# Output strips cut in half and moved in a two-block transformer kernel: half strips ahead of the last head's later sums, the third pair's transposes ahead of the last values

## The chip, the cores and the metric

The kernel runs on one core of a Trainium2 chip. The metric is the device time of one execution in microseconds. The compute engines run their own instruction streams in program order and meet at semaphores: PE (TensorE, matmuls and transposes), DVE (VectorE), ACT (ScalarE) and POOL (GpSimd). SyncE starts the transfers.

## The reference

The reference is a stack of blocks on `x` of 512 rows by 1024 columns. The first block has a convolution layer and a differential attention layer, each with a memory attention and a squared-relu MLP. Its result goes into a second block, where the change is made:

```python
def second_block(x, ...):
    a = _rmsnorm(h, g_pre_mix[l])
    u = jnp.einsum("bsd,dc->bsc", a, w_in[l])
    ...
    conv_out = _conformer_conv(c_val, c_gate, ...)      # GLU, 31 taps, layernorm, silu
    attn_out = _stick_breaking(q, k, v)                 # 8 heads of 64
    attn_out = _rmsnorm(attn_out, attn_norm_g[l]).reshape(B, S, SB_WIDTH)
    mixed = jnp.concatenate([conv_out, attn_out], axis=-1)
    y = jnp.einsum("bsc,cd->bsd", mixed, w_out[l])
    h = h + _rmsnorm(y, g_post_mix[l])
    ...                                                 # gated MLP, second residual

def _stick_breaking(q, k, v):
    # A[t,s] = sigmoid(z_ts) * prod_{s<j<t} (1 - sigmoid(z_tj)), s < t
    ...
    between = lax.cumsum(log_1m_beta, axis=3, reverse=True) - log_1m_beta
    attn = jnp.where(mask, jnp.exp(log_beta + between), 0.0)
    return jnp.einsum("bhqk,bhkd->bhqd", attn, vh)
```

## The kernel before

Every float32 product is made of three matmuls: each operand is split into a rounded high part and a rest, and `mm3` (lines 1060, 1061 and 1062) multiplies high by high, rest by high and high by rest. Matmul sums stand in eight PSUM banks of 128x512 float32.

In the second block the order of work is one list of steps, `PLAN_C`. PE, ACT and DVE each walk the same list, and each does its own share of a step. A step is a name and a number; the order on an engine is that of the list, and semaphores hold an engine where its step needs another's result. The eight heads are units 0 to 7, two heads make a pair. For unit u the steps are:

- `lg` logits on PE; ACT and DVE make the logarithms from them (ACT lines 2099 to 2103, DVE line 2801 in `sp`);
- `sl` ACT rounds the logarithms (line 2108), DVE takes the rest (line 2805);
- `bt` the later sums, `between`, on PE: 20 matmuls (line 1564), the first ten with the rounded part, the others with the rest, added onto the logits in their banks. Even units use banks 0 to 2, odd ones 3 to 5;
- `ex` ACT: exponentials of the three banks (line 2114), counted by semaphore `sb_exp`, three a unit;
- `ah`, `at` ACT rounds the weights (line 2120), DVE takes the rest (line 2809), counted by `at_lo`;
- `va` PE: 12 matmuls of `mm3` into bank 6 (the values); `kp` ACT keeps that head (line 2126) and, after a pair's second head, squares both (line 2130).

For pair p, `ps` sums the squares on PE (line 1617, two columns wide), `pr` and `px` make and spread the norm's factor, `pt` transposes it into bank 7 on PE (line 1622), DVE multiplies it in (line 2824), and `pl` splits the result (ACT line 2145, DVE line 2828, semaphore `pair_lo`).

The convolution's layernorm is woven in: `ln_qa` adds squares on DVE (line 2848), `ln_var` sums them over channels on PE (line 1632, semaphore `ln_q` ahead of it), `ln_mul 0` transposes the factor into bank 7 on PE (line 1637), `ln_mul 1` multiplies it into the four channel groups on DVE (line 2857, four instructions, each read of bank 7 counted by `ln_dve`, from 5 to 8), `silu` and `ll` finish a group.

The output product `w_out_2` is made of strips: a strip is one PSUM bank t (rows 128t to 128t+127), one slab of weights, and two of the eight groups of 128 channels. The first slab holds channel groups 4 and 5, which are pair 0 and pair 1. `o` does strips of that slab, six matmuls each, in banks 0 to 3; `os` those of the next slabs.

Bank 7 is used by several steps in turn. Each of them first waits until the one before has been read, in the order of the list:

```python
        def out_of_7(step):
            ...
            if kind == "pt":
                return S("pair_n"), step[1] + 1
            if kind == "ln_var":
                return S("rs_v"), USE["ln",] + 1
            return S("ln_dve"), 4 if kind == "ln_sub" else 8
```

Of the kernel before, what the change touches and what calls it, by code (L numbers as in the profile page):

```python
# [97 lines left out]
def build(nc, cols, ins, out):  # L98
    sems = {}

    def S(name):
        if name not in sems:
            sems[name] = nc.alloc_semaphore(f"s_{name}")
        return sems[name]
# [18 lines left out]
    banks = [nc.alloc_psum_tensor(f"ps{b}", [128, 512], F32) for b in range(8)]  # L123
# [169 lines left out]
    OUT_KS = [[4, 5], [0, 1], [2, 3], [6, 7]]  # L293
# [326 lines left out]
    PLAN_C = []  # L620
# [12 lines left out]
    for u in range(8):  # L633
# [39 lines left out]
        if u >= 4 and u % 2:  # L673
            PLAN_C += [("pl", u // 2 - 2)]
        PLAN_C += [("taps", 1 if u < 3 else 3)]
    PLAN_C += [("bt", 7), ("ln_qa", 3), ("ps", 2), ("ln_var",), ("va", 6), ("ex", 7), ("pr", 2), ("ln_rs",), ("px", 2),
               ("ah", 7), ("ln_mul", 0), ("at", 7), ("kp", 6), ("ln_mul", 1), ("o", (0, 1)), ("va", 7), ("silu", 0), ("ll", 0),
               ("o", (2,)), ("pt", 2), ("kp", 7), ("ps", 3), ("silu", 1), ("ll", 1), ("o", (3,)), ("silu", 2), ("pl", 2),
               ("ll", 2), ("silu", 3), ("ll", 3), ("w", SL["out", 0, 0] + 4), ("os", 0, 1, (0, 1, 2, 3)), ("pr", 3), ("px", 3),
               ("os", 0, 2, (0, 1)), ("pt", 3), ("pl", 3), ("os", 0, 2, (2, 3))]  # L680

# [201 lines left out]
    M2h, M2l = Ah, Al  # L883
# [163 lines left out]
    def tensor_program(e):  # L1047
        q = Lane(e)
        mm = e.matmul
        at = {"slab": 0}  # L1050

        def next_slab():
            i = at["slab"]
            at["slab"] += 1
            q.wait_ge(S("w_lo"), 2 * i + 2)
            return i, WH[i % N_SPLIT], WL[i % N_SPLIT]

        def mm3(ps, lh, ll, rh, rl, start, stop, skip=False):
            k = dict(skip_group_check=True) if skip else {}
            mm(ps, lh, rh, start=start, stop=False, **k)  # L1060
            mm(ps, lh, rl, start=False, stop=False, **k)  # L1061
            return mm(ps, ll, rh, start=False, stop=stop, **k)  # L1062
# [4 lines left out]
        def tile_t(xh, xl, job, bank, free, turn=no_step, step=no_step):  # L1067

            i, wh, wl = next_slab()
            for k in range(8):  # L1070
                if turn is not no_step:

                    a, k_ = slice(k * 128, k * 128 + 128), dict(skip_group_check=True)
                    q.wait_ge(S("turn_hi"), 8 * JOB[job] + k + 1)
                    if k == 0:
                        free()
                    mm(banks[bank][:, :], wh[:, a], xh[:, k, :], start=k == 0, stop=False, **k_)
                    mm(banks[bank][:, :], wl[:, a], xh[:, k, :], start=False, stop=False, **k_)
                    turn(k)
                    q.wait_ge(S("turn_lo"), 8 * JOB[job] + k + 1)  # L1080
                    m = mm(banks[bank][:, :], wh[:, a], xl[:, k, :], start=False, stop=k == 7, **k_)
                    continue
                q.wait_ge(S("turn_lo"), 8 * JOB[job] + k + 1)
                if k == 0:
                    free()
                m = mm3(banks[bank][:, :], wh[:, k * 128:k * 128 + 128], wl[:, k * 128:k * 128 + 128],
                        xh[:, k, :], xl[:, k, :], k == 0, k == 7)
                if k == 3:
                    step(0)
            m.then_inc(S("w_used"), 1)  # L1090
            step(1)
# [51 lines left out]
        def turn_in_tile(src, job):  # L1143
            return lambda k: turn_next(src, job, 4 + k) if k < 4 else None

        def spread(x, job):
            for t in range(4):
                q.wait_ge(S("rs_n"), 3 * USE[job] + 3)
                i = e.transpose(banks[7][:, 128 * t:128 * t + 128], rms(job, t, 1).broadcast_to([128, 128]), IDENT)
            i.then_inc(S("spread_ps"), 1)  # L1150
# [199 lines left out]
        held, in_use = [], {}  # L1350
# [127 lines left out]
        for p, slot in enumerate(B.plan):  # L1478
            if p == 1:
                row_turn(3, 0)  # L1480
            if p < len(PIECES):
                c, j, t = PIECES[p]
# [22 lines left out]
        def in_free(n):  # L1505
            if n < 4:
                q.wait_ge(*x_final(1, n))
            else:
                q.wait_ge(*in_done(IN_FIRST[n - 4]))

        def v2_slab(j):

            c = CH["v2"]
            _, wh, wl = next_slab()
            for t in range(4):
                if j == 0:
                    q.wait_ge(S("spread"), 4)
                a = slice(128 * t, 128 * t + 128)
                for r, k in enumerate(c.ks[j]):
                    w = slice(512 * r, 512 * r + 512)  # L1520
                    m = mm3(banks[4 + t][:, :], Ah[:, k, a], Al[:, k, a], wh[:, w], wl[:, w], k == 0, k == 7)
                if t == 3:
                    m.then_inc(S("w_used"), 1)
                elif j == 3:
                    m.then_inc(S("n_tile"), 1)

        def free_7(step):

            i = IN_7.index(step)
            if i:  # L1530
                q.wait_ge(*out_of_7(IN_7[i - 1]))
            else:
                q.wait_ge(S("vz_lo"), 4)
# [56 lines left out]
        def block_step(kind, *a):  # L1590
            step = (kind,) + a
            if step in IN_7:
                free_7(step)
            if kind == "tile":
                n = IN_FIRST.index(a[0]) if a[0] in IN_FIRST else -1
                tile_t(Ah, Al, "pre_mix", n % 4 if n >= 0 else 7, lambda: in_free(n) if n >= 0 else None,
                       turn_in_tile(X, "pre_mix") if n == 0 else no_step)
                if n == 0:
                    q.wait_ge(S("turn_lo"), 8 * JOB["pre_mix"] + 8)
                    spread(X, "pre_mix")  # L1600
            elif kind == "v2":
                v2_slab(a[0])
            elif kind == "lg":
                logits(a[0])
            elif kind == "bt":
                between(a[0])
            elif kind == "va":
                values(a[0])
            elif kind == "cv":
                conv_group(a[0])  # L1610
            elif kind == "o":
                out_first(a[0])
            elif kind == "ps":
                q.wait_ge(S("pair_sq"), a[0] + 1)
                q.wait_ge(S("keep"), 2 * a[0] + 2)
                for t in range(4):
                    m = mm(banks[6][:, 2 * t:2 * t + 2], OQ[:, 128 * t:128 * t + 128], HALF[:, :], start=True, stop=True)
                m.then_inc(S("pair_ps"), 1)
            elif kind == "pt":
                q.wait_ge(S("pair_b"), a[0] + 1)  # L1620
                for t in range(4):
                    m = e.transpose(banks[7][:, 128 * t:128 * t + 128], TN[:, 128 * t:128 * t + 128], IDENT)
                m.then_inc(S("pair_t"), 1)
            elif kind == "os":
                out_slab(*a)
            elif kind == "ln_sub":
                q.wait_ge(S("ln_s"), 3)
                mm(banks[7][:, :], ONES, T4[:, 0, :], start=True, stop=True).then_inc(S("ln_ps"), 1)
            elif kind == "ln_var":
                q.wait_ge(S("ln_q"), 7)  # L1630
                for t in range(4):
                    m = mm(banks[7][:, 2 * t:2 * t + 2], GL[:, 0, 128 * t:128 * t + 128], ONES[:, 0:2], start=True, stop=True)
                m.then_inc(S("ln_ps"), 1)
            elif step == ("ln_mul", 0):
                q.wait_ge(S("rs_n"), 3 * USE["ln",] + 3)
                for t in range(4):
                    m = e.transpose(banks[7][:, 128 * t:128 * t + 128], LNR[:, t:t + 1].broadcast_to([128, 128]), IDENT)
                m.then_inc(S("ln_ps"), 1)

        def mixed_ready(k):  # L1640
            if k < 4:
                q.wait_ge(S("mix_lo"), k + 1)
            else:
                q.wait_ge(S("pair_lo"), k - 3)
# [12 lines left out]
        def out_strip(w, j, n, t):  # L1657
            return strip(w, OUT_KS[j], t, 4 * n + t, M2h, M2l, mixed_ready, j == 0, j == 3)

        def out_first(tiles):  # L1660


            if not held:
                held[:] = next_slab()
            for t in tiles:
                q.wait_ge(S("sb_exp"), 21 if t < 3 else 24)
                m = out_strip(held, 0, 0, t)
                if t == 3:
                    m.then_inc(S("w_used"), 1)

        def out_slab(n, j, tiles):

# [25 lines left out]
        for step in PLAN_C:  # L1698
            block_step(*step)
# [37 lines left out]
        for n, j in DN[:3]:  # L1737
            w = next_slab()
            for t in range(4):
                m = down_strip(w, j, n, t)  # L1740
# [1274 lines left out]
```

## Time and profile before

| | |
|---|---|
| median of 3 runs | 1763.02 us (1762.97 to 1763.67) |
| the profiled execution | 1763.04 us |
| its span (first to last instruction) | 1761.2 us |
| PE busy | 1719.3 us, 98% of the span |
| DVE busy, ACT busy | 1256.6 us (71%), 818.4 us (46%) |
| chain that ended last | PE 89%, DVE 6%, ACT 3% |
| mean granted clock of PE | 0.993 |

Times in the rows are microseconds from the start of the span. A timeline row gives start, duration, engine, line, operation, output and input and how many instructions are merged in it; in brackets stands how long the engine had been idle before, and what ended that. Matmuls overlap in the pipeline, so the distance of two starts, and not a duration, is what one costs. The granted clock is 1.00 at 2.4 GHz and 0.50 at 1.2 GHz.

### The profile page before, as it was taken

The numbers are of one execution on the slowest core, as the hardware profiler recorded it, in microseconds if no ns is written. First come the engines' busy times: TensorE is split into PE (matmuls) and PEld (weight loads), VectorE is DVE, ScalarE is ACT, GpSimd is POOL, SyncE is SP. The second block draws the span as 40 slices with busy tenths as digits, with TensorE's granted clock in tenths as the row PEclk, the third lists the DMA queues.
The fourth block names the chain that finished last, engine by engine and source line by source line (L and its number), as shares of the span: only waits on it lengthen the run. The fifth ranks groups of instructions, "written<-read, shape, count | busy, mean of one in ns | idle before, by whom it ended". The sixth has DMA issues, their size and how long they took to land.

```text
span 1761.2 us, 21518 instructions
## 1 busy us (share of the span) xinstructions
PE 1719.3 (98%) x8215; PEld 1416.3 (80%) x8215; DVE 1256.6 (71%) x1915; ACT 818.4 (46%) x1345; POOL 38.0 (2%) x87
## 2 busy tenths in 40 slices
PE   8999999999999999999999999999999999999998
PEld 7887888888888777778888888778888788888886
DVE  6666358687887667775778788889987644765766
ACT  7433244343445656664444343542767532333342
POOL 0000000000001121000000000000000000000000
PEclk9999999999999999999999999999999999999999
DMA  7222442333412112115152423033100353224212
GB/s 250 84 72 84 129 134 80 114 97 106 141 39 65 61 51 71 37 49 180 51 147 66 143 72 120 12 96 101 55 13 7 91 178 96 72 87 143 69 49 84
DMA packets 195749, 158.29 MB, mean 90 GB/s; under 512 B 5248, under 2 KB 161280, under 8 KB 195648
## 3 DMA queue, kind: packets, MB, share of 16 engines
q1 hardware_dynamic: 194240, 154.16, 28.8%
q0 software_dynamic: 400, 1.25, 0.3%
q8 instruction: 65, 1.06, 0.3%
q10 hardware_dynamic: 1008, 1.53, 0.2%
q14 instruction: 36, 0.29, 0.1%
HBM read 154.81 MB, written 2.10 MB: 89 GB/s over the span
## 4 chain that ended last, share of the span: by engine, by line
PE 89%; DVE 6%; ACT 3%; issue 1%; DMA 0%; POOL 0%; DVEq 0%; SPq 0%; ACTq 0%
PE ps L1060 28%; PE ps L1062 28%; PE ps L1061 28%; PE ps L1564 1%; PE ps L1130 1%; ACT sb L2020 1%; DVE sb L2237 1%; ACT sb L1763 1%; PE ps L1453 0%; DVE sb L2494 0%; DVE sb L2235 0%; DVE sb L2263 0%; PE ps L1189 0%; DVE sb L2730 0%; ACT sb L1769 0%
## 5 line engine op out<-in xcount | busy, mean ns | idle before, releaser
L1060 PE MATMUL ps<-sb,sb 128*128 128x512 f32 (+3 forms) x2435 | 928.7, 388 | 9.7 <-ACT sb L2020 5.2
L1062 PE MATMUL ps<-sb,sb 128*128 128x512 f32 (+3 forms) x2435 | 912.6, 380 | 0.0
L1061 PE MATMUL ps<-sb,sb 128*128 128x512 f32 (+3 forms) x2435 | 912.2, 379 | 0.0
L2237 DVE TENSOR_TENSOR sb<-sb,sb 128x1024 fp32r<-128x1024 f32 (+1 forms) x414 | 404.8, 997 | 219.2 <-ACT sb L1763 218.4
L1060 PEld LDWEIGHTS ps<-sb,sb 128*128 128x128 f32 (+1 forms) x2435 | 451.5, 188 | 110.1 <-issue 11.7
L1763 ACT ACTIVATE sb<-sb 128x1024 fp32r<-128x1024 f32 (+1 forms) x414 | 349.7, 871 | 394.5 <-PE ps L1062 389.2
L1062 PEld LDWEIGHTS ps<-sb,sb 128*128 128x128 f32 (+1 forms) x2435 | 451.1, 188 | 86.8
L1061 PEld LDWEIGHTS ps<-sb,sb 128*128 128x128 f32 (+1 forms) x2435 | 451.6, 188 | 82.4 <-issue 0.2
L2477 DVE TENSOR_TENSOR sb<-sb,sb 128x1024 fp32r<-128x1024 f32 x70 | 85.5, 1221 | 47.5 <-ACT sb L1925 45.2
L1920 ACT ACTIVATE sb<-sb 128x512 f32<-128x512 f32 x64 | 40.3, 630 | 130.8 <-DVE sb L2529 130.8
L2459 DVE TENSOR_TENSOR sb<-sb,sb 128x1024 f32<-128x1024 f32 x80 | 95.1, 1216 | 0.6
L2494 DVE TENSOR_TENSOR sb<-ps,sb 128x512 f32<-128x512 f32 x120 | 76.1, 681 | 0.0
L2730 DVE SCALAR_TENSOR_TENSOR sb<-sb,sb,sb 128x512 f32<-128x512 f32 x90 | 67.4, 749 | 1.9
L1925 ACT ACTIVATE sb<-sb 128x1024 fp32r<-128x1024 f32 x56 | 58.7, 1048 | 9.2 <-DVE sb L2471 9.1
L2529 DVE SCALAR_TENSOR_TENSOR sb<-ps,sb 128x512 f32<-128x512 f32 x64 | 43.6, 684 | 9.0 <-PE ps L1062 9.0
L2471 DVE TENSOR_TENSOR sb<-sb 128x1024 f32<-128x1024 f32 x40 | 48.7, 1216 | 0.1
L2193 ACT ACTIVATE sb<-sb 128x512 f32<-128x512 f32 x22 | 13.9, 632 | 72.6 <-DVE sb L2936 72.5
L2263 DVE SCALAR_TENSOR_TENSOR sb<-ps,sb,sb 128x512 fp32r<-128x512 f32 (+1 forms) x48 | 31.0, 700 | 13.6 <-ACT sb L1782 13.6
L2235 DVE SCALAR_TENSOR_TENSOR sb<-sb,sb,sb 128x512 fp32r<-128x512 f32 x40 | 29.5, 747 | 8.8 <-ACT sb L1763 8.5
L1130 PE MATMUL ps<-sb,sb 128*128 128x128 f32 x176 | 27.2, 295 | 8.7 <-DMA sb<-in_con 5.0
L1130 PEld LDWEIGHTS ps<-sb,sb 128*128 128x128 f32 x176 | 22.1, 150 | 14.4 <-DMA sb<-in_con 5.0
L1769 ACT ACTIVATE sb<-sb 128x1024 f32<-128x1024 f32 x26 | 27.6, 1061 | 10.3 <-DVE sb L2684 4.8
(217 smaller groups left out, 1109.3 us busy)
## 6 DMA issues: line engine op xcount, KB each, us to landing
sb<-in_w_up SPq DMA_DIRECT2D x86, 512.0 KB, 4.1
sb<-in_w_down SPq DMA_DIRECT2D x86, 512.0 KB, 4.9
sb<-in_w_gate SPq DMA_DIRECT2D x22, 512.0 KB, 3.9
sb<-in_a_w_in SPq DMA_DIRECT2D x20, 512.0 KB, 3.8
sb<-in_w_in SPq DMA_DIRECT2D x20, 512.0 KB, 3.7
sb<-in_w_o SPq DMA_DIRECT2D x16, 512.0 KB, 3.7
sb<-in_w_mem_kv SPq DMA_DIRECT2D x8, 512.0 KB, 7.6
sb<-in_w_out SPq DMA_DIRECT2D x8, 512.0 KB, 3.8
```

Of the source, the lines that this page charges most:

```text
L1060: mm(ps, lh, rh, start=start, stop=False, **k)
L1061: mm(ps, lh, rl, start=False, stop=False, **k)
L1062: return mm(ps, ll, rh, start=False, stop=stop, **k)
L1130: i = e.transpose(banks[4 + k % 4][:, 128 * t:128 * t + 128], src[:, t, 128 * k:128 * k + 128], IDENT)
L1763: act(WH[i % N_SPLIT][:, a], raw[:, a], ACT.Copy, scale=g).then_inc(S("w_hi"), parts)
L1925: act(AR[(7 * g + j) % 4][0], a_of(l, g, j)[0], ACT.Copy).then_inc(S("h_hi"), 1)
L2237: tt(lo, raw, hi, ALU.subtract).then_inc(S("w_lo"), parts)
L2459: tt(db[d][a][:, :], db[b][a][:, :], db[c][a][:, :], ALU.subtract).then_inc(S("t_sum"), 1)
L2471: tt(d, x, y, op).then_inc(S("hs"), 1)
L2477: tt(lo, a_of(l, g, j)[0], hi.bitcast(F32), ALU.subtract).then_inc(S("h_lo"), 1)
L2494: tt(x, y, x, ALU.add).then_inc(S("res"), 1)
L2730: stt(CV[:, j, :], GL[:, j, k:k + T], col("convw", 4 * k + j), CV[:, j, :], ALU.mult, ALU.add).then_inc(S("tap"), 1)
```

## The change

At the end of `PLAN_C` a step `oa` is new: ahead of `bt 7` it does the first half (channel group 4, pair 0) of strips 0, 1 and 2, nine matmuls, behind a wait for `sb_exp` 21. The step `o` then does only the second half of these strips (channel group 5), all three of them behind `ln_mul 1`, and `pt 2` moves from behind the third strip and `va 7` to behind the three halves and ahead of `va 7`.

```diff
-    PLAN_C += [("bt", 7), ("ln_qa", 3), ("ps", 2), ("ln_var",), ("va", 6), ("ex", 7), ("pr", 2), ("ln_rs",), ("px", 2),
-               ("ah", 7), ("ln_mul", 0), ("at", 7), ("kp", 6), ("ln_mul", 1), ("o", (0, 1)), ("va", 7), ("silu", 0), ("ll", 0),
-               ("o", (2,)), ("pt", 2), ("kp", 7), ("ps", 3), ("silu", 1), ("ll", 1), ("o", (3,)), ("silu", 2), ("pl", 2),
+    PLAN_C += [("oa", (0, 1, 2)), ("bt", 7), ("ln_qa", 3), ("ps", 2), ("ln_var",), ("va", 6), ("ex", 7), ("pr", 2), ("ln_rs",), ("px", 2),
+               ("ah", 7), ("ln_mul", 0), ("at", 7), ("kp", 6), ("ln_mul", 1), ("o", (0, 1, 2)), ("pt", 2), ("va", 7),
+               ("silu", 0), ("ll", 0), ("kp", 7), ("ps", 3), ("silu", 1), ("ll", 1), ("o", (3,)), ("silu", 2), ("pl", 2),
...
+        def out_part(tiles):
+
+            held[:] = next_slab()
+            _, wh, wl = held
+            q.wait_ge(S("sb_exp"), 21)
+            for t in tiles:
+                k, a = OUT_KS[0][0], slice(128 * t, 128 * t + 128)
+                mixed_ready(k)
+                mm3(banks[t][:, :], M2h[:, k, a], M2l[:, k, a], wh[:, 0:512], wl[:, 0:512], True, False)
+
         def out_first(tiles):
 
 
-            if not held:
-                held[:] = next_slab()
             for t in tiles:
-                q.wait_ge(S("sb_exp"), 21 if t < 3 else 24)
-                m = out_strip(held, 0, 0, t)
-                if t == 3:
-                    m.then_inc(S("w_used"), 1)
+                if t < 3:
+                    _, wh, wl = held
+                    k, a = OUT_KS[0][1], slice(128 * t, 128 * t + 128)
+                    mixed_ready(k)
+                    mm3(banks[t][:, :], M2h[:, k, a], M2l[:, k, a], wh[:, 512:1024], wl[:, 512:1024], False, False)
+                else:
+                    q.wait_ge(S("sb_exp"), 24)
+                    out_strip(held, 0, 0, t).then_inc(S("w_used"), 1)
```

On PE, at the end of `va 5` and the start of `bt 7` (the first row is the last matmul of `va 5`, line 1564 is `bt 7`), the difference reads:

```order
 L1062 MATMUL ps<-sb_190,sb_178 128x256
+L1060 MATMUL ps<-sb_60,sb_50 128x512 [waits s_pair_lo,s_sb_exp,s_w_lo]
+L1061 MATMUL ps<-sb_63,sb_50 128x512
+L1062 MATMUL ps<-sb_60,sb_51 128x512
+L1060 MATMUL ps<-sb_60,sb_50 128x512
+L1061 MATMUL ps<-sb_63,sb_50 128x512
+L1062 MATMUL ps<-sb_60,sb_51 128x512
+L1060 MATMUL ps<-sb_60,sb_50 128x512
+L1061 MATMUL ps<-sb_63,sb_50 128x512
+L1062 MATMUL ps<-sb_60,sb_51 128x512
 L1564 MATMUL ps<-sb_188,sb_66 128x256 [waits s_sp_hi]
```

Nine matmuls of 512 columns now stand ahead of `bt 7`, the first of them behind the wait for the exponentials of unit 6.

On PE, the place where `va 7` begins. Before (line 1622 is `pt 2`, line 1617 is `ps 3`; the rows with `sb_60` are strip 2, the row with 128x256 is the last matmul of `va 7`):

```order
6123 L1062 MATMUL ps<-sb_190,sb_178 128x256
6124 L1060 MATMUL ps<-sb_60,sb_50 128x512
6125 L1061 MATMUL ps<-sb_63,sb_50 128x512
6126 L1062 MATMUL ps<-sb_60,sb_51 128x512
6127 L1060 MATMUL ps<-sb_60,sb_50 128x512
6128 L1061 MATMUL ps<-sb_63,sb_50 128x512
6129 L1062 MATMUL ps<-sb_60,sb_51 128x512
6130 L1622 MATMUL ps<-sb_64,sb_78 128x128 [waits s_pair_b,s_ln_dve]
6131 L1622 MATMUL ps<-sb_64,sb_78 128x128 x3
6132 L1617 MATMUL ps<-sb_72,sb_78 128x2 [waits s_keep,s_pair_sq]
```

And of the change (here `pt 2` has line 1624 and `ps 3` line 1619):

```order
6117 L1062 MATMUL ps<-sb_60,sb_51 128x512
6118 L1624 MATMUL ps<-sb_64,sb_78 128x128 [waits s_pair_b,s_ln_dve]
6119 L1624 MATMUL ps<-sb_64,sb_78 128x128 x3
6120 L1060 MATMUL ps<-sb_190,sb_177 128x512 [waits s_keep,s_at_lo]
...
6131 L1062 MATMUL ps<-sb_190,sb_178 128x256
6132 L1619 MATMUL ps<-sb_72,sb_78 128x2 [waits s_keep,s_pair_sq]
```

The transposes of `pt 2`, with their wait for `ln_dve`, now stand ahead of `va 7`, and nothing stands between `va 7` and `ps 3`.

On DVE, the steps from `at 7` (line 2809) on. Before, then of the change (line 2823 is the same instruction as 2809, 2871 as 2857, 2838 as 2824, 2875 as 2861, 2257 as 2243):

```order
1367 L2809 TENSOR_TENSOR sb_191<-sb_187,sb_190 128x1408 [waits s_at_hi]
1368 L2857 TENSOR_TENSOR sb_182<-ps,sb_182 128x512 [waits s_ln_ps]
1369 L2857 TENSOR_TENSOR sb_182<-ps,sb_182 128x512 x3
1370 L2861 TENSOR_TENSOR sb_51<-sb_182,sb_50 128x512 [waits s_mix_hi]
1371 L2824 SCALAR_TENSOR_TENSOR sb_78<-ps,sb_65,sb_193 128x512 [waits s_pair_lo,s_pair_t]
1372 L2243 TENSOR_SCALAR sb_77<-ps 128x8 [waits s_pair_ps]
```

```order
1367 L2823 TENSOR_TENSOR sb_191<-sb_187,sb_190 128x1408 [waits s_at_hi]
1368 L2871 TENSOR_TENSOR sb_182<-ps,sb_182 128x512 [waits s_ln_ps]
1369 L2871 TENSOR_TENSOR sb_182<-ps,sb_182 128x512 x3
1370 L2838 SCALAR_TENSOR_TENSOR sb_78<-ps,sb_65,sb_193 128x512 [waits s_pair_lo,s_pair_t]
1371 L2875 TENSOR_TENSOR sb_51<-sb_182,sb_50 128x512 [waits s_mix_hi]
1372 L2257 TENSOR_SCALAR sb_77<-ps 128x8 [waits s_pair_ps]
```

The multiply of pair 2 has moved ahead of the rest of channel group 0; `at 7` and the four multiplies of `ln_mul 1` keep their places. On ACT the order is the same as before.

## Rows read from the trace of the kernel before

**Rows 1.** Page, busy time of each engine

```profile
PE 1719.3 (98%) x8215; PEld 1416.3 (80%) x8215; DVE 1256.6 (71%) x1915; ACT 818.4 (46%) x1345; POOL 38.0 (2%) x87
```

**Rows 2.** Who PE waited for, 1280 to 1420: total, times, longest

```profile
PE ps L1564 <- ACT sb L2108: 3.6, 1, 3.6
PE ps L1130 <- DVE sb L2890: 2.0, 1, 2.0
```

**Rows 3.** Timeline of PE, 1330 to 1345

```profile
1330.07 3.07 PE L1564 MATMUL ps<-sb,sb 128*128 128x256 f32 x20
1332.98 0.40 PE L1060 MATMUL ps<-sb,sb 128*128 128x512 f32 x1
...
1334.79 0.28 PE L1062 MATMUL ps<-sb,sb 128*128 128x256 f32 x1
1338.67 5.49 PE L1564 MATMUL ps<-sb,sb 128*128 128x256 f32 x20 [3.60 <-ACT sb L2108]
1343.95 1.14 PE L1617 MATMUL ps<-sb,sb 128*128 128x2 f32 x8
1344.95 1.03 PE L1632 MATMUL ps<-sb,sb 128*128 128x2 f32 x8
```

**Rows 4.** Timeline of ACT, 1335 to 1355

```profile
1335.17 1.44 ACT L2114 ACTIVATE sb<-ps 128x512 f32<-128x512 f32 x3
1337.24 1.38 ACT L2108 ACTIVATE sb<-sb 128x1408 fp32r<-128x1408 f32 x1 [0.62 <-DVE sb L2801]
...
1340.53 0.63 ACT L2130 ACTIVATE sb<-sb 128x512 f32<-128x512 f32 x1
...
1348.11 1.38 ACT L2120 ACTIVATE sb<-sb 128x1408 fp32r<-128x1408 f32 x1 [0.79 <-PE ps L1062]
...
1353.44 0.59 ACT L2126 ACTIVATE sb<-ps 64x512 f32<-64x512 f32 x1 [0.18 <-PE ps L1062]
1354.07 0.63 ACT L2130 ACTIVATE sb<-sb 128x512 f32<-128x512 f32 x1
```

**Rows 5.** Timeline of PE, 1345 to 1356

```profile
1345.84 0.48 PE L1060 MATMUL ps<-sb,sb 128*128 128x512 f32 x1
...
1347.85 0.60 PE L1637 MATMUL ps<-sb,sb 128*128 128x128 f32 x4
1348.20 0.48 PE L1060 MATMUL ps<-sb,sb 128*128 128x512 f32 x1
...
1350.36 0.39 PE L1060 MATMUL ps<-sb,sb 128*128 128x512 f32 x1
...
1351.20 0.50 PE L1060 MATMUL ps<-sb,sb 128*128 128x512 f32 x1
...
1353.24 0.40 PE L1060 MATMUL ps<-sb,sb 128*128 128x512 f32 x1
...
1354.61 0.60 PE L1622 MATMUL ps<-sb,sb 128*128 128x128 f32 x4
1355.05 0.95 PE L1617 MATMUL ps<-sb,sb 128*128 128x2 f32 x8
```

**Rows 6.** Timeline of DVE, 1342 to 1354

```profile
1342.33 0.68 DVE L2848 TENSOR_TENSOR sb<-sb 128x512 f32<-128x512 f32 x1
...
1349.52 1.62 DVE L2809 TENSOR_TENSOR sb<-sb,sb 128x1408 fp32r<-128x1408 f32 x1 [2.27 <-ACT sb L2120]
1351.06 2.48 DVE L2857 TENSOR_TENSOR sb<-ps,sb 128x512 f32<-128x512 f32 x4
```

**Rows 7.** Windows: stretch, length, busy (count) of PE, PEld, DVE, ACT, POOL, granted clock, DMA share, GB/s

```profile
1286.40:1289.70 3.30, 3.30 (x24) 3.02 (x24) 3.16 (x6) 2.52 (x5) 0.00 (x0) 1.00 0.53 151
1289.80:1293.10 3.30, 3.30 (x15) 3.20 (x14) 3.30 (x6) 2.03 (x2) 0.00 (x0) 0.50 0.02 8
...
1338.67:1343.95 5.28, 5.28 (x20) 5.09 (x21) 4.34 (x4) 2.96 (x4) 0.00 (x0) 0.50 0.00 0
...
1355.05:1395.90 40.85, 40.85 (x188) 33.90 (x187) 22.08 (x49) 18.73 (x42) 0.58 (x1) 1.00 0.28 78
```

More of the change, by code:

```diff
@@ L1612, in block_step @@
                 out_first(a[0])
+            elif kind == "oa":
+                out_part(a[0])
             elif kind == "ps":
```

## The prediction

> **What bounds the kernel now.** I read the page first: PE is busy for 1719.3 us of the span of 1761.2 [rows 1], so little can be won except where PE stands still or runs slowly. Then the waits of PE around the change: between 1280 and 1420 its largest is a single one of 3.6 us, of line 1564 on ACT's line 2108 [rows 2]. That is `bt 7`, which waits for the rounded logarithms of the last head. The timeline of PE shows the place: the last matmul of `va 5` starts at 1334.79, `bt 7` at 1338.67 after 3.60 idle [rows 3]. The same rows show a second price. `bt 6` starts at 1330.07 and what follows it at 1332.98, so 20 matmuls take 2.91 us; `bt 7` starts at 1338.67 and what follows at 1343.95, which is 5.28 us [rows 3]. The windows say why: the granted clock is 0.50 over all of that stretch, the 1.2 GHz level [rows 7], after an engine that stood still. So the wait costs 3.60 us and 2.37 us after it. From 1355.05 to 1395.90 PE is busy without a gap at a clock of 1.00 [rows 7], so a shift of `ps 3`, which starts at 1355.05 [rows 5], arrives at the end of this block unchanged, and the chain from there to the end is the same code. I therefore follow the change up to the start of `ps 3`.
>
> **The half strips ahead of `bt 7`.** They add no work: nine of the 18 matmuls of three strips move forward. They wait for `sb_exp` 21, the third exponential of unit 6. ACT starts these three at 1335.17 and takes 1.44 [rows 4]: done at 1336.61. PE has been seen to follow ACT by 0.05 (line 2108 ends at 1337.24 + 1.38 = 1338.62, `bt 7` starts at 1338.67) [rows 3, 4], so they start at 1336.66. Nine such matmuls take from 1348.20 to 1350.36, 2.16 us [rows 5]. `bt 7` then starts at 1338.82, 0.15 later than before. The pause shrinks from 3.60 to some 1.6. Their other waits are long met: the weights' slab because no split of weights runs here on DVE [rows 6], pair 0 because it was finished many steps ago.
>
> **The clock of `bt 7`.** The longest pause is now less than half of what preceded the fall. I take full clock: 2.91 instead of 5.28, so PE is through with `bt 7` at 1341.73 instead of 1343.95. Between the ends that the rows give (2.91 and 5.28) I choose the first because 512-column matmuls now fill the second half of the pause.
>
> **How much of that arrives.** `ps 2` needs ACT's squares, 1340.53 + 0.63 = 1341.16 [rows 4]: met. A `ps` took 1.00 at the slow clock [rows 3]; say 0.9, to 1342.63. `ln_var` then waits for the last square sum on DVE, 1342.33 + 0.68 = 1343.01 [rows 6], and starts at 1343.06 instead of 1344.95 [rows 3]. So the gain is cut to 1.89 us: DVE is late next. `va 6` starts 1.89 earlier too, at 1343.95 (before 1345.84 [rows 5]).
>
> From there the chain goes to `ah 7` on ACT (before at 1348.11 [rows 4], now 1346.22), `at 7` on DVE (before 1349.52, now 1347.63) and the four multiplies of `ln_mul 1` (before 1351.06 + 2.48 = 1353.54 [rows 6], now 1351.65). None of these engines has other work in between that the change alters.
>
> **`pt 2` ahead of `va 7`.** Here a wait is added. `pt 2` writes bank 7, whose last reader in the list is `ln_mul`; it waits for `ln_dve` 8, all four multiplies. Before, it came at 1354.61 [rows 5], 1.07 after they ended, and the wait was free. Now PE does `ln_mul 0` (0.35 [rows 5]) at 1345.96 and the nine second halves (2.16), so it reaches `pt 2` at 1348.47 and waits until 1351.70: 3.1 us idle. Behind it in PE's queue stands `va 7`, whose own weights are ready at the end of `at 7`, at 1349.25; for `va 7` wait ACT (`kp 7`), and through it `ps 3`.
>
> Then, at full clock: `pt 2` 0.44 [rows 5], `va 7` from 1352.14. Before, `va 7` started at 1351.20 and ACT's line 2126 at 1353.44, 2.24 later [rows 4, 5]; now 1354.38. The squares follow 0.63 later and take 0.63 [rows 4]: 1355.64. **Cover lost:** before, the third strip (1353.24 to 1354.61) and `pt 2` (to 1355.05) [rows 5], 1.81 us of PE work, lay over this piece of ACT work. Now nothing stands between `va 7` and `ps 3`, and PE idles another 1.3 us. `ps 3` starts at 1355.70 instead of 1355.05: 0.65 later, with no clock lost.
>
> On DVE the multiply of pair 2 goes ahead of `ll 0`, 0.7 us that nobody waits for, as the strips of channel groups 0 and 1 come only after strip 3. ACT's order, POOL and the transfers are untouched: no queue is passed.
>
> **The clock at the new pauses.** PE idles 3.1 us, works some 2.4, idles 1.3, and then has the two-column matmuls of `ps 3`. That 3.60 idle preceded a fall is shown [rows 3, 7]; and from 1289.80 the clock was 0.50 for 3.3 us after a stretch in which PE never stood still at all [rows 7], one of 64-row matmuls and of `ps` columns. Bounds: nothing; or all of `va 7` at half clock (12 matmuls from 1351.20 to 1353.24, 2.04 us more [rows 5]) and one such stretch of 3.3 us of dense strips afterwards (1.65 more). The new pause is close to the old one, so I take half of each: 1.02 + 0.83 = 1.85. The Trainium skill's page "TensorE: Matmul & The Clock Gate" (section "HAM oscillation — how this bites in real kernels") says that long waits between bursts of matmuls make each burst begin throttled; by that rule this change only moves the throttled burst from `bt 7` to `va 7`. If only the old, longer pause were long enough in the page's sense, nothing would be lost and the time would be that of rival 1.
>
> **The sum** against the profiled execution's 1763.04 (the median of the runs is 1763.02, the same): -1.89 (what is left of the pause's and the clock's gain), +2.54 (waits for `ln_dve` 8 and for the squares; the two make +0.65), +1.85 (clock) = +2.50, so 1765.5 us.
>
> **The rivals.**
> 1. No fall of the clock at the new pauses, 0.65 alone: 1763.7. For it: the pause is shorter than the 3.60. Against: not by much, and a second follows within 3 us. 22%.
> 2. The full price: both stretches at half clock, 0.65 + 2.04 + 1.65 = +4.3: 1767.4. For it: each term has been seen once. It lies above the bound of 0.2% (3.5 us), which is about what a measurement of this kernel can tell from no change. 25%.
> 3. `bt 7` stays slow in spite of the half strips: then all is 0.15 later than before up to `ln_mul 1` (1353.69), `ps 3` starts at 1357.7, +2.7, and with half the clock's price +4.5: 1767.5. Against: the pause is more than halved. 8%.
> 4. The other side: the wait for `ln_dve` 8 does not bite, `pt 2` runs at 1348.47 and `va 7` at 1349.30 after `at 7`, and `ps 3` starts 3.56 later at 1352.9: -2.2, 1760.8. It decides if the last multiply of `ln_mul 1` ends by 1348.5; the rows put it at 1351.65, three microseconds too late, and DVE can't start it before `at 7`. 3%.
>
> **How the numbers follow.** My own case, part of the clock's price paid, has 42%, for 1764.3 to 1766.5. The likeliest time is 1765.5. The range from 1763.4 (just below rival 1) to 1767.4 (rival 2) leaves out rival 4, half of rival 3 and the far side of rival 2. Slower by over 0.2% are most of rival 2 and rival 3: 28%. Faster by over 0.2% needs more than rival 4 gives: 2%. The rest, 70%, lies within 0.2%.
>
> **What the changed profile would show.** Right: `bt 7` starting near 1338.8 behind some 1.6 idle and taking 2.9; `ln_var` starting near 1343.1; a wait of PE's transposes for DVE's multiplies of 3 us ending near 1351.7; then `ps 3` waiting for ACT's squares over 1 us; a granted clock of 0.50 in a part of 1350 to 1361. Wrong: `bt 7` at 5.3 us; or `pt 2` without a wait; or `ps 3` starting before 1355.0. What would make the number wrong is above all where the clock falls and how long it stays down: it alone moves it by 3.7 us.

## The result: the change is some 4.7 us slower, as a difference just above the range's upper end

Over 14 executions each, the change takes a median of 1765.2 us (1762.57 to 1770.05) and the kernel before 1761.55 us (1758.94 to 1763.69). The ratio is 1.0027, with a 95% interval of 1.0019 to 1.0034: between 3.3 and 6.0 us slower. The forecast of 1765.5 lies beside the median, but partly by luck, since it was made against an execution of 1763.04 and the kernel before turned out 1.5 us faster in its median. As a difference the forecast was +2.5 us and the measured one is +4.7, above the +4.4 of the range's upper end and above 0.2% (its interval begins at 0.19%): the case that had 28%, not the one that had 70%. Its size is less sure than its sign. Four of the 14 executions of the change took 1768.1 to 1770.1 us at mean clocks of 0.990 to 0.992, the other ten 1762.6 to 1765.5, so the means differ by 4.5 us and the medians by 3.7.

The profiled execution of the change took 1764.59 us, its span is 1762.8 us. First its waits, as PE had them between 1280 and 1420 (total, times, longest), against [rows 2]:

```profile
PE ps L1624 <- DVE sb L2871: 2.4, 1, 2.4
PE ps L1130 <- DVE sb L2904: 2.0, 1, 2.0
PE ps L1060 <- issue: 1.7, 1, 1.7
PE ps L1077 <- ACT sb L1796: 1.4, 1, 1.4
PE ps L1619 <- ACT sb L2144: 1.3, 1, 1.3
PE ps L1634 <- DVE sb L2862: 0.4, 1, 0.4
```

The wait of 3.6 us ahead of `bt 7` has gone and 1.7 ahead of the half strips is what is left of it. Two waits are new: 2.4 us of `pt 2` (line 1624) for the multiplies of `ln_mul 1` (2871), and 1.3 us of `ps 3` (1619) for ACT's squares (2144). `ln_var` (1634) waits 0.4 for DVE's last square sum. All four were in the prediction; the 2.0 and the 1.4 stand after this block, where the kernel before waits 2.0 and 1.6. The timeline of PE at these places, against [rows 3, 5]:

```profile
1334.93 0.47 PE L1060 MATMUL ps<-sb,sb 128*128 128x512 f32 x1 [1.66 <-issue]
...
1337.09 3.13 PE L1564 MATMUL ps<-sb,sb 128*128 128x256 f32 x20
1340.06 0.95 PE L1619 MATMUL ps<-sb,sb 128*128 128x2 f32 x8
1341.38 1.02 PE L1634 MATMUL ps<-sb,sb 128*128 128x2 f32 x8 [0.37 <-DVE sb L2862]
1342.26 0.48 PE L1060 MATMUL ps<-sb,sb 128*128 128x512 f32 x1
...
1345.18 1.05 PE L1639 MATMUL ps<-sb,sb 128*128 128x128 f32 x4
...
1350.96 0.66 PE L1624 MATMUL ps<-sb,sb 128*128 128x128 f32 x4 [2.43 <-DVE sb L2871]
...
1354.88 1.05 PE L1619 MATMUL ps<-sb,sb 128*128 128x2 f32 x8 [1.34 <-ACT sb L2144]
```

`bt 7` takes 2.97 us from start to next start (before 5.28). But `va 6`, from 1342.26 to 1345.18, takes 2.92 (before 2.01). The windows of the change show the clock behind that:

```profile
1342.26:1345.18 2.92, 2.92 (x15) 2.78 (x15) 1.06 (x7) 1.04 (x3) 0.00 (x0) 0.66 0.00 0
1348.50:1350.90 2.40, 0.03 (x1) 0.00 (x0) 2.40 (x5) 1.58 (x3) 0.00 (x0) 1.00 0.00 0
1354.88:1356.80 1.92, 1.92 (x12) 1.75 (x13) 0.74 (x2) 1.89 (x3) 0.00 (x0) 1.00 0.00 0
1356.90:1360.20 3.30, 3.30 (x10) 2.56 (x9) 2.01 (x4) 3.22 (x6) 0.00 (x0) 0.50 0.03 5
```

The granted clock is down in `va 6` (0.66 on average) and then at 0.50 over 3.3 us of the dense strips behind `ps 3`. In `pt 2` and the new `va 7` it was at full level in this execution, although PE had just idled 2.43.

The slow `va 6` does not shorten the wait of `pt 2`, since the chain to the multiplies starts with it. ACT's rounding of the weights (`ah 7`, here line 2134) waits for the last matmul of `va 6`:

```profile
1345.47 1.38 ACT L2134 ACTIVATE sb<-sb 128x1408 fp32r<-128x1408 f32 x1 [1.73 <-PE ps L1062]
```

PE and the multiplies are both late by the 0.91 us of `va 6`. What cuts the wait from the expected 3.1 to 2.4 is the work behind it: from the first transpose of `ln_mul 0` to the last of the nine matmuls of the second halves it is 2.96 us here (1345.18 to 1348.14) and 2.28 for the same 13 instructions before (1347.85 to 1350.13), because the clock was still down for a part of them.

**The ledger of the two profiles.** I count from the start of ACT's rounding for head 7, which nothing in the change touches. Before it is at 1337.24 [rows 4], and in the change here:

```profile
1335.45 1.38 ACT L2122 ACTIVATE sb<-sb 128x1408 fp32r<-128x1408 f32 x1 [0.61 <-DVE sb L2815]
```

So the change came 1.79 us early into this stretch, for a reason outside it: before, the clock was down from 1289.80 to 1293.10 [rows 7], and in this execution of the change it was not. From there to `ps 3` it is 17.81 us before and 19.43 in the change, +1.62. From `ps 3` to the first transposes after this block it is 40.85 before (1355.05 to 1395.90) and 42.58 in the change, +1.73, the fall behind `ps 3`; the transposes of the change are here:

```profile
1397.46 1.15 PE L1130 MATMUL ps<-sb,sb 128*128 128x128 f32 x9
```

-1.79 + 1.62 + 1.73 = +1.56, and the spans differ by 1.6. What the change did in these two executions is thus +3.35 us; the 1.79 it seemed to save belongs to a fall of the clock elsewhere, which one execution had and the other had not.

### The profile page after: what moved, and what is told of

Read it like the earlier page. It is cut to its first block, busy times and chain, and to the rows that moved or that the text cites. A ratio compares the mean times of both kernels' runs of the same rounds, so it can differ in the third digit from the quotient of the medians.

```text
span 1762.8 us, 21518 instructions
## 1 busy us (share of the span) xinstructions
PE 1719.2 (98%) x8215; PEld 1415.4 (80%) x8215; DVE 1256.7 (71%) x1915; ACT 818.8 (46%) x1345; POOL 38.0 (2%) x87
## 4 chain that ended last, share of the span: by engine, by line
PE 89%; DVE 6%; ACT 3%; issue 1%; DMA 0%; POOL 0%; DVEq 0%; SPq 0%; ACTq 0%
PE ps L1060 28%; PE ps L1062 28%; PE ps L1061 28%; PE ps L1130 1%; PE ps L1564 1%; ACT sb L2034 1%; PE ps L1453 1%; ACT sb L1777 1%; DVE sb L2251 0%; DVE sb L2508 0%; DVE sb L2249 0%; PE ps L1077 0%; PE ps L1189 0%; PE ps L1081 0%; PE ps L1078 0%
```

## The experiments

The kernel before ran beside each of them, again and again; its median was 1761.58 (33 runs) beside the first four, 1761.53 (35) beside the next four and 1759.39 (21) beside the last two. That is why ratios are given, with their 95% intervals, and why a median of one group isn't set against one of another. The means of the kernel before beside the change, the first four and the next four are within 0.05 us of each other (1761.52, 1761.53, 1761.57), so means of these kernels can be compared. One execution moves by 2 to 4 us with the clock: of the 33, those of mean clock 0.996 took 1758.8 to 1759.6 us, those of 0.993 1762.9 to 1763.6.

The last column is the ledger's own measure: in the one profiled execution of each kernel, the time from the start of ACT's rounding for head 7 to the first transposes after this block, less the 58.66 us of the kernel before (1337.24 to 1395.90). Falls of the clock elsewhere are left out of it, those inside the block are in it.

| kernel | median us (runs) | ratio to before | interval | block in the profile, us |
|---|---|---|---|---|
| the change | 1765.2 (14) | 1.0027 | 1.0019 to 1.0034 | +3.35 |
| half strips alone | 1761.18 (11) | 0.9996 | 0.9987 to 1.0005 | -1.23 |
| order around `va 7` alone | 1765.35 (11) | 1.0017 | 1.0006 to 1.0027 | +2.50 |
| change, `pt 2` behind `va 7` | 1761.66 (11) | 0.9994 | 0.9985 to 1.0003 | -0.43 |
| change, `pt 2` in bank 5 | 1761.31 (11) | 0.9999 | 0.9991 to 1.0008 | -0.40 |
| change, pauses filled | 1765.49 (12) | 1.0013 | 1.0004 to 1.0022 | +2.34 |
| before, pause filled | 1761.51 (11) | 1.0000 | 0.9991 to 1.0008 | -0.31 |
| strip 3 ahead of the sums | 1760.49 (11) | 0.9995 | 0.9986 to 1.0003 | -1.42 |
| change, strip 3 as cover | 1761.47 (11) | 1.0006 | 0.9997 to 1.0014 | +2.86 |
| strip 3, half strip between sums | 1759.07 (11) | 0.9992 | 0.9983 to 1.0001 | -2.64 |
| before, pauses filled twice | 1761.24 (11) | 1.0008 | 1.0000 to 1.0017 | -1.37 |

**The two parts apart.** First only the half strips, the rest of the order as before:

```diff
-... ("ln_mul", 1), ("o", (0, 1, 2)), ("pt", 2), ("va", 7),
-               ("silu", 0), ("ll", 0), ("kp", 7), ("ps", 3), ...
+... ("ln_mul", 1), ("o", (0, 1)), ("va", 7), ("silu", 0), ("ll", 0),
+               ("o", (2,)), ("pt", 2), ("kp", 7), ("ps", 3), ...
```

> One part of the change alone: the nine half matmuls ahead of bt 7, then the old order (two strips ahead of va 7, the third strip and pt 2 behind it). Theory (the loss is the wait of pt 2 for the multiplies and the lost cover of ACT's squares, plus clock falls that these pauses bring): bt 7 takes 2.9 us, PE waits some 1.5 us for at 7, and ps 3 comes about 2.2 us earlier than before; total 1.5 to 3 us faster than the kernel before. Rival (splitting the strips itself costs, or the half strips hold up bt 7): slower than before by 1 us or more.

0.9996 (-2.3 to +0.9 us): no loss of 1 us or more, so splitting strips costs nothing that can be seen; the gain of some 2.2 us is not seen either, only just inside the interval. The profile shows where a part of it stays. `bt 7` is fast, and then `va 6` is slow:

```profile
1342.66:1345.39 2.73, 2.73 (x15) 2.59 (x14) 1.06 (x7) 1.04 (x3) 0.00 (x0) 0.71 0.00 0
1345.39:1352.33 6.94, 6.19 (x31) 4.92 (x30) 4.80 (x7) 5.87 (x8) 0.00 (x0) 0.87 0.00 0
```

The second window goes to `ps 3`. From ACT's rounding to `ps 3` this profile has 16.48 us (1335.85 to 1352.33) against 17.81: 1.33 won where 2.2 were expected.

Then only the other part, in the kernel before:

```diff
-... ("ln_mul", 1), ("o", (0, 1)), ("va", 7), ("silu", 0), ("ll", 0),
-               ("o", (2,)), ("pt", 2), ("kp", 7), ("ps", 3), ...
+... ("ln_mul", 1), ("o", (0, 1, 2)), ("pt", 2), ("va", 7),
+               ("silu", 0), ("ll", 0), ("kp", 7), ("ps", 3), ...
```

> The other part alone: no half strips; three whole strips and pt 2 ahead of va 7. Theory: bt 7 stays at half clock after the 3.6 us pause; PE reaches pt 2 some 1.2 us before the last multiply, waits, and then waits 1.3 us for ACT's squares behind va 7: ps 3 about 2.5 us later, total 2.5 to 4.5 us slower than before. Rival (only the clock's falls make the change slow): within 1 us of before, since the pause ahead of bt 7 and its fall are there already.

1.0017 (+1.1 to +4.8 us): a loss sits in this part. Its waits, in which the old pause is back and both new ones stand beside it:

```profile
PE ps L1564 <- ACT sb L2108: 3.6, 1, 3.6
PE ps L1130 <- DVE sb L2890: 2.0, 1, 2.0
PE ps L1077 <- ACT sb L1782: 1.4, 1, 1.4
PE ps L1617 <- ACT sb L2130: 1.3, 1, 1.3
PE ps L1622 <- DVE sb L2857: 1.0, 1, 1.0
```

1.0 us ahead of `pt 2` (expected 1.2) and 1.3 for the squares, as expected. Behind its slow `bt 7` the clock did not fall again in this block:

```profile
1346.10:1355.78 9.68, 7.30 (x40) 5.89 (x38) 5.37 (x7) 5.86 (x8) 0.00 (x0) 1.00 0.00 0
1355.78:1395.00 39.22, 39.22 (x179) 32.62 (x180) 19.70 (x45) 18.34 (x40) 0.58 (x1) 1.00 0.28 81
```

The rival, that only falls of the clock make the change slow, fails: `bt 7` has its fall here as before, no other is added, and the block is 2.50 us longer from the waits alone. The two parts also act on each other. Here PE waits 1.0 us at `pt 2`, in the change 2.4 (and 3.07 in a kernel below): the nine half matmuls, 2.16 us, that fill the old pause are missing ahead of `pt 2`, and since the end of the multiplies is set by DVE and not by the strips, the pause opens again there.

**The wait for bank 7.** Two kernels take away what `pt 2` waits for. In one it stands behind `va 7` again, by which time the multiplies are all but done:

```diff
-... ("o", (0, 1, 2)), ("pt", 2), ("va", 7), ("silu", 0), ("ll", 0), ("kp", 7), ...
+... ("o", (0, 1, 2)), ("va", 7), ("silu", 0), ("ll", 0), ("pt", 2), ("kp", 7), ...
```

> The change with one step undone: pt 2 stands behind va 7 again (no strip between va 7 and ps 3). Theory: the 2.4 us wait of PE for the multiplies is replaced by a wait of under 1 us for at 7; ps 3 comes some 2 us earlier than before, 1 to 2.5 us faster than before, 4 to 6 faster than the change. Rival (lost cover behind va 7 is the main loss): stays 2 us or more slower than before.

In the other the order is the change's own, but these four transposes go to bank 5, and DVE reads them there:

```diff
+                if a[0] == 2:
+                    q.wait_ge(S("sb_exp"), 24)
                 for t in range(4):
-                    m = e.transpose(banks[7][:, 128 * t:128 * t + 128], TN[...], IDENT)
+                    m = e.transpose(banks[5 if a[0] == 2 else 7][:, 128 * t:128 * t + 128], TN[...], IDENT)
```

> The change in its own order, but pt 2 transposes into bank 5, which is free after the last exponentials, in place of bank 7, so that it need not wait for the multiplies of ln_mul 1. Theory (the wait for bank 7 is what costs): as with pt 2 behind va 7, 1 to 2.5 us faster than before. Rival (the place of pt 2 matters in itself, for example through DVE's order): no better than the change.

0.9994 (-2.6 to +0.5 us) and 0.9999 (-1.6 to +1.4 us): each gives back the loss of the change within these bounds, 4.5 us from mean to mean in bank 5, and neither is shown to beat the kernel before, where both expectations had a gain of 1 to 2.5 us. Both rivals fail. The second is the cleaner proof, since not one instruction changes its place, only a bank and the wait that goes with it; the uncovered squares stay in it. In its profile `pt 2` runs at once, and `va 7` waits 0.24 us for its own weights:

```profile
1346.50 0.60 PE L1626 MATMUL ps<-sb,sb 128*128 128x128 f32 x4
1347.34 0.50 PE L1060 MATMUL ps<-sb,sb 128*128 128x512 f32 x1 [0.24 <-DVE sb L2825]
...
1350.88 1.05 PE L1619 MATMUL ps<-sb,sb 128*128 128x2 f32 x8 [1.34 <-ACT sb L2146]
```

ACT's rounding started at 1335.16, so `ps 3` came 15.72 us later, 2.1 sooner than before and as much as both expectations said (with `pt 2` behind `va 7` it was 0.5 sooner, with a slow `va 6`). Most of it was lost again in this execution: a fall of the clock to 0.50 followed behind `ps 3`, from 1352.1 to 1355.3:

```profile
1341.97:1343.99 2.02, 2.02 (x15) 1.88 (x15) 1.05 (x7) 1.04 (x3) 0.00 (x0) 1.00 0.00 0
1343.99:1350.88 6.89, 5.31 (x31) 4.30 (x30) 5.22 (x7) 5.87 (x8) 0.00 (x0) 1.00 0.00 0
1350.88:1352.00 1.12, 1.12 (x9) 1.12 (x10) 0.08 (x2) 1.09 (x2) 0.00 (x0) 1.00 0.00 0
1352.10:1355.30 3.20, 3.20 (x9) 2.43 (x8) 1.92 (x4) 3.14 (x6) 0.00 (x0) 0.50 0.03 5
```

The first window is `va 6` at full clock, 2.02 us. So the clock fell in `va 6` in one execution, behind `ps 3` in another, and in both places in the change's.

**The lost cover.** Strip 3 is put over ACT's squares, `pt 2` stays where the change has it:

```diff
-... ("pt", 2), ("va", 7), ("silu", 0), ("ll", 0), ("kp", 7), ("ps", 3), ("silu", 1), ("ll", 1), ("o", (3,)), ...
+... ("pt", 2), ("va", 7), ("silu", 0), ("ll", 0), ("o", (3,)), ("kp", 7), ("ps", 3), ("silu", 1), ("ll", 1), ...
```

> The change with pt 2 left ahead of va 7, but the whole strip 3 moved between va 7 and ps 3, so that it lies over ACT's squares. Theory (the lost cover costs 1.3 us, the wait for the multiplies the rest): 1.3 to 2 us faster than the change, still slower than before by 1.5 to 3.5 us. Rival (the uncovered squares cost nothing, or are the main loss): as slow as the change, or as fast as before.

1.0006 (-0.5 to +2.5 us), where the change has 1.0027. The means differ by 3.6 us (by an estimate from the spread of the executions, 1.9 to 5.3), likely more than the 1.3 to 2 expected. In its profile PE waits the full 3.07 us ahead of `pt 2` and no longer for the squares:

```profile
1353.65 0.66 PE L1624 MATMUL ps<-sb,sb 128*128 128x128 f32 x4 [3.07 <-DVE sb L2871]
...
1359.01 0.98 PE L1619 MATMUL ps<-sb,sb 128*128 128x2 f32 x8
```

That alone would explain 1.3. The rest might be the clock, with strip 3 as dense work behind the pause, but this profile does not bear that out. `va 6`, the wait and what follows it:

```profile
1344.44:1347.90 3.46, 3.46 (x13) 3.17 (x14) 1.05 (x7) 1.04 (x3) 0.00 (x0) 0.54 0.00 0
1350.60:1353.60 3.00, 0.00 (x0) 0.00 (x0) 2.99 (x5) 2.17 (x3) 0.00 (x0) 1.00 0.00 0
1353.65:1359.00 5.35, 5.35 (x22) 4.68 (x23) 1.35 (x2) 1.34 (x3) 0.00 (x0) 0.68 0.00 0
```

Behind the wait, in `va 7` and so ahead of strip 3, the clock fell again, and the block is 2.86 us longer than before. It is also the slowest of the 11 executions (1766.16 us, the fastest 1760.45), so it is not the typical one. The two remedies do not add up: bank 5 takes away the one wait and gives back 4.5 us, strip 3 takes away the other and gives back 3.6, of a loss of 4.5. Each was nearly enough alone, and what the wait for bank 7 costs when the squares are covered is not shown to differ from nothing.

**The clock in the new pauses.** Spare matmuls whose sums are never read keep PE busy in both pauses of the change:

```diff
+            elif kind == "fill":
+                q.wait_ge(S("sb_exp" if a[0] == 4 else "pair_n"), 24 if a[0] == 4 else 2)
+                mixed_ready(4)
+                for i in range(a[1]):
+                    mm(banks[a[0]][:, :], M2h[:, 4, 0:128], M2h[:, 4, :], start=True, stop=True, skip_group_check=True)
...
-... ("pt", 2), ("va", 7), ...
+... ("fill", 4, 11), ("pt", 2), ("va", 7), ("fill", 4, 6), ...
```

> The change with PE kept busy in its two new pauses: 11 spare matmuls of 512 columns into bank 4 ahead of pt 2 (2.5 us, shorter than the pause) and 6 behind va 7 (1.4 us). They are extra work and their sums are never read. Theory (part of the loss is a clock that falls because of these pauses): 1.5 to 3 us faster than the change although it does more work, mean clock 0.995 or above, still 1.5 to 3 us slower than before. Rival (the clock plays no part, only waits do): not faster than the change, and the second filler adds 0 to 0.3 us.

1.0013 against 1.0027, with more work in it: means of 1764.19 (12 runs) and 1766.04 (14 runs), mean clocks of 0.9948 and 0.9931. Against the kernel before, 2.3 us (0.7 to 3.9) of the loss stays. The profile has its fall in `va 6` and none in the former pauses or behind `ps 3`:

```profile
1344.40:1347.90 3.50, 3.50 (x15) 3.20 (x14) 1.05 (x7) 1.04 (x3) 0.00 (x0) 0.53 0.00 0
1347.90:1357.60 9.70, 9.17 (x47) 7.32 (x46) 5.37 (x7) 5.84 (x8) 0.00 (x0) 0.99 0.00 0
1357.60:1365.00 7.40, 7.40 (x37) 6.26 (x37) 3.66 (x7) 7.24 (x12) 0.00 (x0) 1.00 0.01 2
```

The means put the clock's share at 1.9 us, but the size is not secured: an estimate from the spread of the executions gives 0.2 to 3.6, and the medians (1765.49 and 1765.2) show no gain at all. What differs is that none of the 12 executions lies above 1766.3, while four of the change's 14 lie above 1768. That a part of the loss is clock is likely by this and by the profiles; how large it is stays open.

**Where the gain of `bt 7` went.** The kernel before, with only its own pause filled by 13 spare matmuls into bank 7 (`("fill", 7, 13)` ahead of `("bt", 7)`):

> The kernel before with 13 spare matmuls of 512 columns into bank 7 ahead of bt 7 (3.0 us in a pause of 3.6; their sums are never read), nothing else changed. Theory: bt 7 takes 2.9 us instead of 5.3, PE then waits for the last square sum and for at 7, ps 3 comes 1.3 to 1.9 us earlier; the total is 0.5 to 1.9 us faster than before, because the clock can fall a little later in the narrow matmuls of ps 2 and ln_var, as it did with the half strips alone. Rival (the gain of the half strips was the 2 us of work taken out of the later stretch, not the clock): no change against before.

1.0000: nothing, the time that the rival had. Its windows are `bt 7`, the two groups of narrow matmuls, and `va 6`:

```profile
1337.13:1340.31 3.18, 3.18 (x20) 2.90 (x21) 3.18 (x3) 2.96 (x4) 0.00 (x0) 1.00 0.00 0
1340.31:1342.40 2.09, 1.82 (x18) 1.73 (x16) 1.24 (x3) 1.77 (x5) 0.00 (x0) 1.00 0.00 0
1342.40:1345.90 3.50, 3.50 (x14) 3.22 (x14) 1.05 (x7) 1.04 (x3) 0.00 (x0) 0.52 0.00 0
```

`bt 7` gains 2.1 us, and `va 6`, right behind `ps 2` and `ln_var` with their two columns, takes 3.5 instead of 2.0. Together with the wait of `ln_var` for DVE, the gain is all but spent when `va 6` is over: ACT's rounding starts at 1335.70 here and the transposes behind `va 6` at 1346.00, 10.30 us later, before 10.61 (1337.24 to 1347.85). To test that link, 4 more spare matmuls went between `ps 2` and `ln_var` (`("fill", 7, 4)`):

> The kernel before with the 13 spare matmuls ahead of bt 7 and 4 more of 512 columns (0.9 us, bank 7, sums never read) between ps 2 and ln_var, where PE waits 0.3 us. Theory (the clock's gain at bt 7 is given back in va 6): va 6 runs at 1.00 in spite of 0.6 us of work added to the path; 0.5 to 1.5 us faster than before, where 13 alone gave nothing. Rival (no link with the narrow matmuls): 0.3 to 0.8 us slower than with the 13 alone, the fall in va 6 remains.

```profile
1341.88:1344.52 2.64, 2.64 (x23) 2.46 (x21) 1.27 (x3) 1.77 (x5) 0.00 (x0) 1.00 0.00 0
1344.52:1346.52 2.00, 2.00 (x14) 1.87 (x14) 1.06 (x7) 1.04 (x3) 0.00 (x0) 1.00 0.00 0
```

`va 6` is back at 2.00 us and a clock of 1.00, and the block is 1.1 us shorter than with the 13 alone. The theory's time, though, is missed: 1.0008 (0 to +3.0 us), no gain, on the side of a loss and nearer to the rival's time. The mechanism is seen in the profile, a profit of it in the total is not.

**Better orders.** Half strips ahead of `bt 7`, three second halves, `va 7`, then strip 3 and `pt 2` over ACT's squares:

```diff
+... ("ln_mul", 1), ("o", (0, 1, 2)), ("va", 7),
+               ("silu", 0), ("ll", 0), ("o", (3,)), ("pt", 2), ("kp", 7), ("ps", 3), ("silu", 1), ("ll", 1), ("silu", 2), ...
```

> Half strips ahead of bt 7, three second halves ahead of va 7, and behind va 7 the whole strip 3 and then pt 2, ahead of ps 3: every wait of the change gets cover. Theory: PE waits 0.7 us for at 7 and not for the multiplies nor the squares; ps 3 starts some 1.9 us earlier than before and is followed directly by the next slab, so that slab starts about 3 us earlier; total 1.5 to 3 us faster than before. Rival (what limits is now the silu chain that makes channel groups 0 and 1): the next slab waits for it, less than 1 us faster than before.

0.9995 (-2.5 to +0.5 us), not shown to be a gain. The profile has no wait ahead of the next slabs, so it does not show the rival's silu chain, but its `va 6` was slow again (3.37 us). And with the second half of strip 0 moved between `ps 2` and `ln_var` (`("ps", 2), ("o", (0,)), ("ln_var",)`, and then `("o", (1, 2))`):

> As with strip 3 ahead of ps 3, and the second half of strip 0 (three matmuls of 512 columns, 0.7 us) stands between ps 2 and ln_var, two groups of two-column matmuls behind which the clock fell in va 6 in five profiles. Theory (the regained clock of bt 7 is given back there, because PE has little to do between bt 7 and va 6): the clock stays at 1.00 through va 6, the mean clock rises to 0.996 or above, and the total is 2 to 3.5 us faster than before. Rival (the falls in va 6 have nothing to do with the narrow matmuls): the same as without this move, 1 to 2 us faster than before, with the fall in va 6 still in the profile.

0.9992 (-3.0 to +0.2 us), short of the 2 to 3.5 us expected; the mean clock is 0.996 as expected, and the two windows, sums and `va 6`, are at full clock (without such work between the sums, `va 6` was slow in seven profiles, not five, and fast in one):

```profile
1342.07:1344.47 2.40, 2.40 (x22) 2.27 (x20) 1.25 (x3) 1.77 (x5) 0.00 (x0) 1.00 0.00 0
1344.47:1346.48 2.01, 2.01 (x14) 1.88 (x14) 1.06 (x7) 1.04 (x3) 0.00 (x0) 1.00 0.00 0
```

In this profile PE has only one wait between `bt 7` and the next slabs, 1.4 us ahead of `va 7`, and the whole block, from ACT's rounding to the transposes behind it, takes 56.02 us, 2.64 less than before:

```profile
1337.46 1.39 ACT L2122 ACTIVATE sb<-sb 128x1408 fp32r<-128x1408 f32 x1 [0.61 <-DVE sb L2815]
...
1393.48 1.14 PE L1130 MATMUL ps<-sb,sb 128*128 128x128 f32 x9
```

This kernel has the lowest ratio of the study, and it can't be told from the kernel before with certainty.

## Why the prediction was right and where it was off

- **The half strips and `bt 7`: right.** Predicted 1.6 idle and 2.91 us; measured 1.66 and 2.97, and not one execution profiled with something dense in that pause had a slow `bt 7` (2.97 to 3.18 us in ten profiles).
- **"How much of that arrives": the term that was mis-sized.** I took 1.89 us. The cut by DVE's last square sum was there (0.37 us of wait). What I missed is that `va 6` stood next in line for the fall: it took 2.92 us in the change's profile where I had 2.01, so that about 1.0 of the 1.89 arrived. Over many executions the same shows: filling the old pause alone gives 0.0 (0.9991 to 1.0008), and the half strips alone 0.7 with an interval that reaches across zero. The working took the clock as spared once it was spared at `bt 7`. [Rows 7] held the warning, a fall after a stretch of `ps` columns with no pause at all, and I used it only for the new pauses.
- **`pt 2` ahead of `va 7`: right in kind and place.** Predicted 3.1 us of idle; 2.43 in the change's profile, where the slow transposes and halves behind `va 6` ate 0.7 of it, and 3.07 where those ran at full clock. Bank 5 shows that this wait is enough to cause the loss together with the uncovered squares; with the squares covered it is not shown to cost anything.
- **Cover lost behind `va 7`: right.** 1.3 predicted, 1.34 measured.
- **The clock at the new pauses: right in size in the profile, +1.85 against 1.73,** though I had half of it in `va 7` and half in the strips. In the change's profile `va 7` ran at full clock after 2.43 us of idle, and the whole fall came behind `ps 3`; with strip 3 as cover it came in `va 7`, after 3.07. Taking half of two bounds was a guess that came near. Over many executions this term is not measured: 0.2 to 3.6.
- **The sum.** -1.89 + 2.54 + 1.85 = +2.5. In the two profiles the first two make +1.62 and not +0.65, of which `va 6` is 0.91, and with the clock's 1.73 that is +3.35. With the first term at the measured -0.0 to -0.7, the same sum gives +3.7 to +4.4; the first lies at the lower edge of the measured +3.3 to +6.0, the second inside. What sets the four slowest executions of the change apart is not known beyond their lower mean clock, as none of them was profiled. Rivals 2 (+4.3) and 3 (+4.5) were nearest in size, but not for their reasons: `va 7` was fast in the change's profile, and so was `bt 7`. Rival 4 fails, as `pt 2` did wait, and rival 1's +0.65 lies below the interval. That the time of 1765.5 comes so near the median of 1765.2 is luck: a difference some 2 us too small on a kernel before that was measured 1.5 us too slow.
- **The rule of the Trainium skill** ("TensorE: Matmul & The Clock Gate", "HAM oscillation — how this bites in real kernels"), by which this change would only move the throttled burst: the trace agrees in that the burst moved, to behind `ps 3` after the two new waits. It differs in `va 6`, which was slow with no long wait ahead of it: 0.37 us at `ln_var`, and 1.66 ahead of the half strips, with `bt 7` at full clock in between.

What stays open: how large the clock's part of the loss is; why either remedy alone gives back nearly all of it; and whether the last kernel wins the 2.64 us of its profile in most executions, since 0.9992 plus or minus 0.0009 allows that as well as nothing. The kernel before with both fillers warns against counting on it: its block was 1.37 us shorter in the profile and its total no shorter.

## What to carry to other kernels

Before moving a step forward on the engine that bounds the kernel, look up every semaphore that the step waits for at its new place, also the one that guards its buffer: a step that waits for free because it stands late becomes the head of the queue when it stands early, and all behind it waits with it. When work is moved off a place, ask what wait it was covering; here 1.8 us of strips and transposes lay over 1.3 us of another engine's squares. And a clock regained in one place can be lost in the next: look in the new profile for where the fall went instead, here to behind the two-column matmuls and the new waits.

## What the runs showed of the hardware

The granted clock fell with PE busy without a gap, or nearly so, behind matmuls two columns wide. It was down in `va 6`, behind `ps 2` and `ln_var`, in seven of the eight profiles in which dense work stood ahead of `bt 7` and none between these two (2.73 to 3.57 us for `va 6`); only with `pt 2` in bank 5 did it hold there (2.02 us). In both kernels in which 0.7 to 0.9 us of 512-column matmuls stood between the two, it held, in the one execution of each that was profiled. After 2.43 us of idle in one execution it was still at full level, after 3.07 in another it was at 0.50 within `va 7`, and after 3.60 it was at 0.50 in `bt 7`. The executions of one kernel on one core spread by 5 us (the kernel before, 1758.8 to 1763.8) in step with their mean clock, 0.996 to 0.992; eleven executions beside 33 of the kernel before gave an interval of about 1.6 us to either side.
